# Stick-breaking weights: split and stored in the first stage, or loaded raw and split on GpSimd beside the heads

## What is computed

```python
h = layer_norm(x, ln0_g, ln0_b)
proj = h @ w_in[l]                      # 1024 -> 4096 columns
qa, ka, va, qb, kb, vb, gate = split(proj)
ya = dilated_mixture(heads_a(qa), heads_a(ka), heads_a(va), rel_bias)
yb = stick_breaking(heads_b(qb), heads_b(kb), heads_b(vb))
y = concatenate([ya, yb]) * silu(gate)
h = layer_norm(DEEPNORM_ALPHA * h + y @ w_out[l] + b_out[l], ln_g[l], ln_b[l])

# stick breaking: causal, z = q k / sqrt(64)
a = exp(log_sigmoid(z) + reverse cumulative sum of log_sigmoid(-z) over later keys)
out = a @ v
```

## Time and profile before

| | |
|---|---|
| median of 3 runs | 1634.42 us (1634.22 to 1635.87) |
| the profiled execution: its time | 1635.06 us |
| its span, first to last instruction | 1633.3 us |
| mean granted PE clock | 0.996 |
| PE busy | 1598.9 us, 98% |
| DVE / ACT / POOL busy | 1112.2 / 727.5 / 382.1 us |
| first stage on PE | to 493.3 us |
| stick-breaking stage on PE | 493.3 to 1139.7 us |
| moved by DMA | 295.55 MB |

### The profile page before, as it was taken

One profiled execution on the slowest core, in us unless ns is written; L12 is line 12 of the kernel. 1 busy time (PEld: TensorE's weight loads), 2 busy tenths in 40 slices (PEclk: granted clock), 3 DMA queues, 4 the chain that ended last, 5 costly groups with the idle time before them and its releaser, 6 DMA issues.

```text
span 1633.3 us, 26457 instructions
## 1 busy us (share of the span) xinstructions
PE 1598.9 (98%) x9102; PEld 1376.3 (84%) x9102; DVE 1112.2 (68%) x2188; ACT 727.5 (45%) x1788; POOL 382.1 (23%) x236
## 2 busy tenths in 40 slices
PE   5999999999999999999999999999999999999997
PEld 4777888888888888888888888887999999987886
DVE  5731124322227888888888888888678787878888
ACT  5541113201224555555555555555677667641000
POOL 2200000000000111111111111012577778761232
PEclk9999999999999999999999999999999999999999
DMA  5434666645659564945485548532667777465542
GB/s 182 154 120 117 219 232 229 209 145 170 217 198 283 181 197 147 285 161 181 164 270 168 181 153 236 165 127 77 192 157 205 191 203 197 137 204 187 166 153 78
DMA packets 183052, 295.55 MB, mean 181 GB/s; under 512 B 51801, under 2 KB 108500, under 8 KB 178132
## 3 DMA queue, kind: packets, MB, share of 16 engines
q1 hardware_dynamic: 180756, 294.01, 58.1%
q10 hardware_dynamic: 2080, 0.01, 0.1%
q0 software_dynamic: 96, 0.04, 0.0%
HBM read 185.66 MB, written 104.01 MB: 177 GB/s over the span
## 4 chain that ended last, share of the span: by engine, by line
PE 88%; DVE 4%; DMA 3%; SPq 1%; POOL 1%; issue 1%; ACT 1%; DVEq 0%; ACTq 0%; POOLq 0%
PE proj L385 25%; PE proj_a L1074 16%; PE out_ps L1898 7%; PE wt_ps L1043 7%; PE oa_ps L1461 6%; PE z_ps L1033 4%; PE o_ps L1059 4%; PE z_ps L1032 4%; PE o_ps L1057 4%; PE pt_ps L1442 3%; PE s_ps L1433 3%; PE s_ps L1434 2%; SPq L1351 1%; DMA b_col<-in_ln_b 1%; PE vtp L407 1%
## 5 line engine op out<-in xcount | busy, mean ns | idle before, releaser
L1097 ACT ACTIVATE z_ps<-z_ps 128x512 f32<-128x512 f32 (+2 forms) x320 | 165.8, 518 | 277.1 <-PE z_ps L1033 276.9
L1152 DVE TENSOR_TENSOR_SCAN W<-z_ps,W,zeros 128x512 f32<-128x512 f32 x192 | 245.8, 1280 | 55.4 <-ACT z_ps L1097 55.0
L385 PE MATMUL proj<-h_hi,w_hi 128*128 128x512 f32 x608 | 243.9, 401 | 4.9 <-DVE h_lo L565 3.7
L385 PE MATMUL proj<-h_hi,w_lo 128*128 128x512 f32 x608 | 238.0, 391 | 0.0
L385 PE MATMUL proj<-h_lo,w_hi 128*128 128x512 f32 x608 | 237.4, 390 | 0.0
L1495 ACT ACTIVATE prob<-neg_s,rows 128x256 f32<-128x256 f32 (+1 forms) x384 | 173.6, 453 | 89.7 <-DVE rows L1542 89.0
L1160 DVE TENSOR_TENSOR WT_lo<-wt_ps,WT_hi 128x512 fp32r<-128x512 f32 (+1 forms) x320 | 187.7, 587 | 5.9 <-ACT WT_hi L1105 5.9
L1105 ACT ACTIVATE WT_hi<-wt_ps 128x512 fp32r<-128x512 f32 (+1 forms) x320 | 169.9, 531 | 10.8 <-PE wt_ps L1043 9.3
L1043 PE MATMUL wt_ps<-ident,W 128*128 128x128 f32 x1088 | 171.9, 273 | 0.1
L1542 DVE CUSTOM_DVE_ANT_0 neg_s<-s_ps,h_lo 128x256 f32<-128x256 f32 (+1 forms) x384 | 122.9, 363 | 63.9 <-PE s_ps L1434 54.5
L1011 POOL TENSOR_TENSOR y_sum<-y_sum,ends 64x512 f32<-64x512 f32 x32 | 33.1, 1033 | 565.0 <-DVE y_sum L1167 565.0
(11 more groups left out here) (196 smaller groups left out, 3136.1 us busy)
## 6 DMA issues: line engine op xcount, KB each, us to landing
wa_hi<-wa_d SPq DMA_DIRECT2D x48, 512.0 KB, 3.7
wa_lo<-wa_d SPq DMA_DIRECT2D x48, 512.0 KB, 4.8
wa_d<-x_sb SPq DMA_DIRECT2D x24, 512.0 KB, 3.7
va_d<-st SPq DMA_DIRECT2D x48, 256.0 KB, 2.7
va<-va_d SPq DMA_DIRECT2D x12, 1024.0 KB, 8.5
w_raw<-in_w_tiles SPq DMA_DIRECT2D x18, 512.0 KB, 5.0
x_sb<-in_x SPq DMA_DIRECT2D x16, 512.0 KB, 5.5
qk_hi_d<-st SPq DMA_DIRECT2D x32, 256.0 KB, 2.6
```

The lines of the kernel that those rows point to most:

```text
L385: last = pe.matmul(acc_of(n)[:], w[w_slot(t)][:, k, :], h[ch][:, k, :], start=(k, a) == (0, 0), stop=(k, a) == (KD - 1, 2))
L1097: act.activation(z_ps[n % Z_SLOTS][:, 0:width], z_ps[n % Z_SLOTS][:, 0:width], ACT.Sigmoid, scale=-SCALE).then_inc(w_done, 1)
L1152: dve.tensor_tensor_scan(W[n % W_SLOTS][:, 0:width][:, ::-1], z_ps[n % Z_SLOTS][:, 0:width][:, ::-1], above[:, ::-1], first, ALU.mult, ALU ...
```

## The change

The 12 weight tiles are no longer loaded, split and stored in the first stage, and `wa_d` is gone. Instead `load_wa(a)` of the second stage loads one raw tile of 512 KB from the input into the single buffer `wa_raw`, once for each of the 48 groups, and POOL splits it into `wa_hi` and `wa_lo` by a copy and a subtraction. PE waits for the split instead of the load. A load waits until the split before it is done; a split waits for its load and, from a = 2 on, until the group that used its slot is done. POOL does splits 0 and 1 before the q_lo zeros, and before each y_sum those splits whose load stands ahead of that result's store in SP's plan. On SP's queue load_wa(1) moves up, directly behind load_wa(0). Two further waits are new on DVE: for the last stores of the first stage before the first low part (step 8), and for its own last sum before the dilated heads. `o_low` moves to another address, and `gap_ends` shrinks.

```diff
--- before.py
+++ after.py
@@ front_phase
-    A_AT, A_SLOTS = (36, 38, 40, 42, 44, 46, 66, 68, 70, 72, 74, 76), 4
...
-            def load_wa(a):
-                if a == 0:
-                    sp.wait_ge(toe_sent, 16 * 3)
-                if a >= A_SLOTS:
-                    sp.wait_ge(wa_stored[a % A_SLOTS], 32 * (a // A_SLOTS))
-                sp.dma_start(wa_slot(a, 0), w_tiles[W_TILES + a]).then_inc(wa_loaded[a % A_SLOTS], 16)
-
-            def store_wa(a):
-                sp.wait_ge(wa_split, a + 1)
-                for part in range(2):
-                    sp.dma_start(wa_d[a, part], wa_slot(a, 1 - part)).then_inc(wa_stored[a % A_SLOTS], 16)
...
-                if n in A_AT:
-                    a = A_AT.index(n)
-                    act.wait_ge(wa_loaded[a % A_SLOTS], 16 * (a // A_SLOTS + 1))
-                    act.activation(wa_slot(a, 1).bitcast(F32R), wa_slot(a, 0), ACT.Copy).then_inc(wa_hi_done, 1)
...
-                if n in A_AT:
-                    a = A_AT.index(n)
-                    dve.wait_ge(wa_hi_done, a + 1)
-                    dve.tensor_tensor(wa_slot(a, 0).bitcast(F32R), wa_slot(a, 0), wa_slot(a, 1),
-                                      ALU.subtract).then_inc(wa_split, 1)
@@ stick_phase
+        o_low = m.ring("o_low", 2, [DH, CH])
+        m.sb("gap_ends", [P, 384])
...
+        wa_raw = m.sb("wa_raw", [P, KD, P])
...
             def load_wa(a):
-                if a >= 2:
-                    sp.wait_ge(a_done, a - 1)
-                for part, tile in enumerate((wa_hi, wa_lo)):
-                    sp.dma_start(tile[a % 2][:].bitcast(F32), wa_d[a % A_TILES, part]).then_inc(wa_loaded[a % 2], 16)
+                if a >= 1:
+                    sp.wait_ge(wa_split, a)
+                sp.dma_start(wa_raw[:], w_tiles[W_TILES + a % A_TILES]).then_inc(wa_loaded, 16)
...
-            for slot in range(3):
-                sp.wait_ge(front.wa_stored[slot], front.wa_counts)
+            sp.wait_ge(*front.toe_free)
             load_wa(0)
+            load_wa(1)
             load_k(0, 0)
-            sp.wait_ge(front.wa_stored[3], front.wa_counts)
             load_q(0)
             sp.dma_start(ones_above[:], mask).then_inc(mask_loaded, 16)
-            load_wa(1)
             load_k(0, 1)
             load_q(1)
             front.close(sp)
@@ stick_phase, gpsimd
-            pool.wait_ge(front.wa_stored[3], front.wa_counts)
+            def split_wa(a):
+                pool.wait_ge(wa_loaded, 16 * (a + 1))
+                if a >= 2:
+                    pool.wait_ge(a_done, a - 1)
+                pool.tensor_copy(wa_hi[a % 2][:], wa_raw[:]).then_inc(wa_hi_done, 1)
+                pool.wait_ge(wa_hi_done, a + 1)
+                pool.tensor_tensor(wa_lo[a % 2][:], wa_raw[:], wa_hi[a % 2][:].bitcast(F32),
+                                   ALU.subtract).then_inc(wa_split, 1)
+
+            pool.wait_ge(*front.toe_free)
+            split_wa(0)
+            split_wa(1)
+            pool.wait_ge(wa_split, 2)
             pool.wait_ge(front.w_split, front.w_tiles)
             for slot in range(Q_SLOTS):
                 pool.memset(q_lo0[slot][DH:P, :].bitcast(F32), 0.0).then_inc(q_zeros_set, 1)
+            pool.wait_ge(q_zeros_set, Q_SLOTS)
+            split = 2
             for n in range(GROUPS):
+                if n >= 1:
+                    pool.wait_ge(y_done, n)
+                while split < A_GROUPS and A_END[split - 2] + 1 <= LAST[n] + VALUES_LAG + 3:
+                    split_wa(split)
+                    split += 1
+                pool.wait_ge(wa_split, split)
@@ stick_phase, tensor
-                        pe.wait_ge(wa_loaded[a % 2], 32 * (a // 2 + 1))
+                        pe.wait_ge(wa_split, a + 1)
@@ stick_phase, vector
+                if s == LOW_LAG:
+                    for landed, count in front.stores:
+                        dve.wait_ge(landed, count)
@@ dilated_phase, vector
             dve.sem_inc(gated, 2)
+            dve.wait_ge(*stick.results)
```

More of the change, by code:

```diff
@@ L120, in front_phase @@
 def front_phase(nc, block, x, w_tiles, ln_g, ln_b, rel_bias, onehot, toe_d, qk_hi_d, qk_lo_d, gate_d, va_d, dv_d,
-                vend_d, wa_d, h_d, toe_sent, ident, mv, rstd, h_hi, h_lo):
+                vend_d, h_d, toe_sent, ident, mv, rstd, h_hi, h_lo):
     LEAD = 3
@@ L262, in settle @@
             sp.wait_ge(h_stored, 16 * 4)
-            for slot in range(A_SLOTS):
-                sp.wait_ge(wa_stored[slot], 32 * A_TILES // A_SLOTS)
         @block.sync
@@ L330, in _ @@
                     store_h((n - H_FIRST) // 4)
[L331 to L335, removed]
                 if n == VB_LAST + 3:
@@ L638, in _, with __init__ @@
                     second(n)
-                if n in A_AT:
-                    a = A_AT.index(n)
-                    dve.wait_ge(wa_hi_done, a + 1)
-                    dve.tensor_tensor(wa_slot(a, 0).bitcast(F32R), wa_slot(a, 0), wa_slot(a, 1),
-                                      ALU.subtract).then_inc(wa_split, 1)
-        return FrontEnd(m.semaphores, close, settle, second_done, len(GROUPS), h_stored, wa_stored,
-                        32 * A_TILES // A_SLOTS, w_split, W_TILES)
+        toe_free = (toe_sent, 16 * 3)
+        return FrontEnd(m.semaphores, close, settle, second_done, len(GROUPS), h_stored, toe_free, w_split, W_TILES,
+                        [(st_stored[slot], stored_by(len(GROUPS) - ST_SLOTS + slot)) for slot in range(ST_SLOTS)])
 class FrontEnd:
-    def __init__(self, spent, close, settle, second_done, groups, h_stored, wa_stored, wa_counts, w_split, w_tiles):
+    def __init__(self, spent, close, settle, second_done, groups, h_stored, toe_free, w_split, w_tiles, stores):
         self.spent, self.close, self.settle = spent, close, settle
@@ L654, in __init__ @@
         self.h_stored, self.h_count = h_stored, 16 * 4
-        self.wa_stored, self.wa_counts = wa_stored, wa_counts
+        self.toe_free = toe_free
         self.w_split, self.w_tiles = w_split, w_tiles
+        self.stores = stores
 class StickEnd:
@@ L732, in load_bias, with stick_phase @@
                 .then_inc(self.bias_loaded[par], 16)
-def stick_phase(nc, block, front, heads, a_stored, y_stored, h_hi, h_lo, wa_d, h_d, qk_hi_d, qk_lo_d, gate_d, dv_d, vend_d,
+def stick_phase(nc, block, front, heads, a_stored, y_stored, h_hi, h_lo, w_tiles, h_d, qk_hi_d, qk_lo_d, gate_d, dv_d, vend_d,
                 toe_d, mask, ident, y_d):
@@ L2119, in build @@
     y_d = nc.dram_tensor("y_d", [2 * WIDTH, T], F32)
-    wa_d = nc.dram_tensor("wa_d", [A_TILES, 2, P, KD, P], F32)
     h_d = nc.dram_tensor("h_d", [2, 2, P, KD, CH], F32)
@@ L2139, in build @@
                         front_end = front_phase(nc, block, x, w_tiles, ln0_g, ln0_b, rel_bias, onehot, toe_d, qk_hi_d, qk_lo_d,
-                                                gate_d, va_d, dv_d, vend_d, wa_d, h_d, toe_sent, ident, mv, rstd, front_hi,
+                                                gate_d, va_d, dv_d, vend_d, h_d, toe_sent, ident, mv, rstd, front_hi,
                                                 front_lo)
@@ L2144, in build @@
                     a_stored, b_stored = between.sems("a_stored", 2), between.sems("b_y_stored", 2)
-                    stick_end = stick_phase(nc, block, front_end, heads, a_stored, b_stored, h_hi, h_lo, wa_d, h_d, qk_hi_d,
+                    stick_end = stick_phase(nc, block, front_end, heads, a_stored, b_stored, h_hi, h_lo, w_tiles, h_d, qk_hi_d,
                                             qk_lo_d, gate_d, dv_d, vend_d, toe_d, mask, ident, y_d)
```

10 lines of the change are left out of this document (3 added, 7 removed).

## The result

The kernel after takes 1668.53 us (median of 4 runs, 1666.63 to 1676.83), the kernel before 1634.34 (4 runs, 1634.22 to 1635.87) beside it: ratio 1.0217, 95% interval 1.0182 to 1.0251. Slower, as forecast, but by 34.2 us instead of 4.2, and far outside the range.

A forecast was written before the change was run, and what follows sets the result against it. PE bounds both stages, so only the opening costs: two waits, 2.0 and 2.2 us, all else 0, sum +4.2 us on the median 1634.42 gives 1638.6 us; range 1635.0 to 1643.0.

The forecast's parts named there:

- The opening: Where PE passes from the first to the stick-breaking stage: PE ends up +4.2 us late, at least +2, at most +7.
- the second wait: PE waits 2.2 us more at group 3, near 522 us, for POOL's split of a late load.
- the clock drop that I had as a rival: Opening: the granted clock drops after PE's pause at 499 us; +7.6 us, 1642.0, chance 0.10.
- step 4: Opening, group 3: load issued at 515.6, split by 524.3, PE 4.2 us late in all; the two waits don't add.
- The splits: 48 splits added on idle POOL: 3.5 us each, 168 us in all; upper bound 4.4 us a split.
- The first stage: Removing twelve pairs of splits, 27 us of ACT and DVE work, and their DMAs beside a full PE: worth 0.
- Contention: Stick-breaking stage: POOL's work does not slow DVE's scans, 0 us; rival of blocked DVE +78 us, 1713, chance 0.03.
- In the middle ... Cost 0: Mid stick-breaking stage: 3.7 us landing plus 3.5 us split fit in a group's 13.3 us, so PE loses 0.
- A rival named late splits: Mid stick-breaking stage: landings over 9.8 us in crowded groups make splits late; a few us, about 1643, chance 0.04.
- The small ones: DVE's new waits, 0 at step 8 and 0 to 0.1 us entering the dilated stage; POOL's self-waits under 0.1 us each.
- The border: Slow clock from 1142 to 1150 us stays; rival: it goes, saving 3.4 us, so +0.8, 1635.2, chance 0.09.

## Why the prediction was wrong

- **The opening: right in its waits and its size, the size in part by luck.** PE's wait before the first score was forecast at 2.0 us and took 2.1, group 3's lateness at 4.2 us and came to 4.4, group 4 then 4.5. load_wa(3) was issued at 515.01 (forecast 515.6) and split by 524.4 (524.3). But the second wait was 1.1 us instead of 2.2, because the clock drop that I had as a rival did come behind the first wait, for 1.7 us. So PE would have been 4.1 us late without any second wait, as the run with the loads moved up shows, and SP's chain gave 4.4 in this profile and 6.1 in that with 11 empty instructions, whose opening is the same. The two don't add, as step 4 has it, and the rival's +7.6 did not come.
- **The splits: right.** 1.04 and 2.40 us on POOL, the first of the two bounds. **The first stage: right**, worth 0. **Contention: right.** Of the 192 scans of 128x512 on a W column the 32 that ran wholly beside a split of POOL took 1.279 us on average, the 124 that touched none 1.280. (The scan of the earlier trace rows ran beside POOL's addition for 0.98 of its 1.28 us, not wholly.) A scan reads one operand from PSUM and one from SBUF, so the Trainium skill's rule on two SBUF inputs (SBUF — State Buffer, Who interferes with whom) did not bind here.
- **"In the middle ... Cost 0": wrong, 12 us.** I let the load go out "when group a is done". By its only semaphore, the split before it, it may go even sooner; it goes out when SP gets to it, and a later sentence of the same paragraph had the reason in hand: "POOL's y_sum work comes up to one split later". I covered that with two buffers of y_sum, which is the cover of DVE that writes it, and never asked who waits for it on the other side: SP, whose store_y stands ahead of load_wa. At group 26 the slot was free at 827.7, when group 24's last matmul ended, and the issue came at 832.50. The landing took 9.1 us; from 827.7 that and a split of 3.5 would have ended at 840.3, in time by 1.5. With the landing of 3.7 that I had counted on, the late issue would have ended in time too, by 2.1. So it took both, and the landings were the second thing sized too small: in this stage they ran from 3.5 to 10.4 (median 4.9). A rival named late splits, but at a few us and 0.04, as a matter of landings alone. The kernel with the load moved up in SP's order shows the 12 us gone; it does not part SP's stand at y_sum from the load's late place in the plan.
- **"The small ones", dilated stage 0 to 0.1: wrong, 17 us.** I looked there only for semaphores. The profile of before had the row, DVE 2.66 us at "issue", and PE's stock covered it, so I did not price what a longer pause would do. The change takes the 12 subtractions out of DVE's program and puts one instruction for the new waits in, 11 less in sum, and so moves the loop's head over a border of the instruction fetch. Most of the price is not the pause (3.6 us of waits) but the clock behind it (13.6 us). I had priced a clock drop in the opening alone, and at 3.4 us.
- **The border**: the drop did not go away, 3.5 us in both profiles, as the forecast had it. In the one execution with the zeros first it did (1.00), so the rival can happen.

By the numbers the sum should have been 4.4 + 12.1 + 17.8 = 34.3. The forecast got the direction by the opening, which is an eighth of the loss; two terms that it put at nothing made the rest.

## What to carry to other kernels

Work that is moved onto an idle engine lengthens the latency of its queue, and whoever waits for anything behind it: follow each result of that engine to the in-order queue that stores or reloads it, and price a load from the moment when the queue reaches it. A change in the number of instructions ahead of a loop can move its head over a fetch border; where a profile shows a pause with no releaser at a jump back, look in that window for transfers on the instruction queues and measure the change also with a few empty instructions, or what is measured is the place. With queue and place mended the change still took 0.17 to 0.33% longer than the kernel before in four kernels. In the three with the opening mended too the interval is clear of 1, and none of the four beats the kernel before.

## What the runs showed of the hardware

- DVE's pause at a jump back takes 2.4 to 2.8 us or 4.5 to 5.4, with nothing between in any kernel run: one or two instruction transfers of 8192 bytes. A shift of 5 instructions, from 1986 to 1991, decides which.
- A pause of PE of 1.5 to 2.3 us in the dilated stage, with 5.37 of 8 us busy in the kernel after, is followed by some 10 to 14 us at 0.50, which costs 5.1 to 6.8 us; once, with the loads earlier, it was 11.9. In the stick-breaking stage a wait of 2.1 us was followed by 1.7 us lost in 4, one of 3.4 us by 1.7 lost in 8, one of 3.8 by 3.4, and one of 2.0 (11 empty instructions, group 3) by none. What makes the drop in the dilated stage the longer one was not found.
- The low clock at the border between the two stages costs 0 to 3.5 us in ten profiles (0 with the zeros first), and 10.5 to 16.8 in four. These four are the kernels with the whole opening mended (0.76, 0.76, 0.85, 0.85). Why was not found. Their runs scatter by up to 13 us, and the slower ones have the lower mean clock; where the clock was low in the runs without a profile is not known. The kernel before scattered as widely on one chip (19 runs, 1631.77 to 1645.17 us).
